# TensorE's overflow branch ahead of the last expert's products, which then stand in both arms

## The reference

```
expert_id = g_top * EXPERTS_PER_GROUP + top_i
combine = jnp.sum(jax.nn.one_hot(expert_id, N_EXPERTS, dtype=jnp.float32) * w[..., None], axis=1)
hid = jax.nn.silu(jnp.einsum('td,edf->etf', t, w_gate)) * jnp.einsum('td,edf->etf', t, w_up)
hid = hid * combine.T.astype(hid.dtype)[:, :, None]
y = jnp.einsum('etf,efd->td', hid, w_down)
x = first_block(...)                      # ends with x + y
return second_block(x, ...)               # begins with rmsnorm(h, g_pre)
```

## Time and profile before

| | |
|---|---|
| median of 3 runs | 1380.82 us (1379.18 to 1384.27) |
| the profiled execution's own time | 1392.52 us |
| its span, first to last instruction | 1391.2 us |
| PE busy / weight loads busy | 1324.2 us (95%) / 800.8 us (58%) |
| DVE / ACT / POOL busy | 571.5 / 338.8 / 477.2 us |
| mean granted TensorE clock | 0.985 |
| matmuls, weight loads | 10076, 10076 |
| the branch | 812.9 us into the span |

### The profile page before, as it was taken

The page is one execution under the profiler, slowest core; times in us unless marked ns, Lnnn a source line. Parts: engine busy times, 40 slices in busy tenths (PEclk is TensorE's granted clock), DMA queues, the critical chain, the costliest instruction groups (busy, mean ns, idle before and its releaser), DMA issues. The chain is left out here.

```text
span 1391.2 us, 24035 instructions
## 1 busy us (share of the span) xinstructions
PE 1324.2 (95%) x10076; PEld 800.8 (58%) x10076; DVE 571.5 (41%) x1381; ACT 338.8 (24%) x788; POOL 477.2 (34%) x586
## 2 busy tenths in 40 slices
PE   6999998999999979999999979999999999999997
PEld 5876445788887454434444425467677445655443
DVE  4366126841415254222111143462388571343315
ACT  2225126631010110111111133462212201322221
POOL 7667603774634800212222302053241011111061
PEclk9999999999999989999999989999999999999999
DMA  8191315021312686999999942011312332200221
GB/s 265 60 382 63 91 61 186 1 65 61 122 61 79 226 302 237 372 360 380 381 378 381 367 176 76 8 61 61 116 67 60 93 106 77 78 2 17 78 105 61
DMA packets 100369, 213.07 MB, mean 153 GB/s; under 512 B 14677, under 2 KB 22704, under 8 KB 100128
## 3 DMA queue, kind: packets, MB, share of 16 engines
q1 hardware_dynamic: 87728, 173.49, 34.9%
q0 software_dynamic: 12528, 37.97, 8.1%
HBM read 190.98 MB, written 19.42 MB: 151 GB/s over the span
## 5 line engine op out<-in xcount | busy, mean ns | idle before, releaser
L1589 POOL TENSOR_TENSOR AR<-Wt,AR 128x512 f32<-128x512 f32 x68 | 88.6, 1323 | 99.1 <-PE pb L1788 93.3
L3932 PE MATMUL pb<-Wt,HT 128*128 128x512 f32 x256 | 117.8, 602 | 0.5 <-DVE AR L4023 0.5
L2480 PE MATMUL pb<-AR 128*64 128x512 f32 x256 | 85.0, 595 | 0.7 <-issue 0.7
L2687 POOL DMA_DIRECT2D ys<-AR x28 | 15.1, 543 | 189.7 <-ACT AR L2651 189.7
L3932 PEld LDWEIGHTS pb<-Wt,HT 128*128 128x128 f32 x256 | 46.3, 190 | 52.4 <-issue 49.3
L1788 PE MATMUL pb<-AR 128*128 128x256 f32 x320 | 73.2, 380 | 1.9 <-DVE AR L1995 1.2
L2480 PE MATMUL pb<-Wt,AR 128*64 128x512 f32 x192 | 70.8, 595 | 0.0
L1788 PEld LDWEIGHTS pb<-AR 128*128 128x128 f32 x320 | 60.2, 190 | 11.5 <-issue 2.0
L1589 POOL TENSOR_TENSOR AR<-Wt 128x512 f32<-128x512 f32 x34 | 44.2, 1320 | 65.1 <-DMA Wt<-in_w_in_dram 30.7
L1788 PE MATMUL pb<-HT,Wt 128*128 128x256 f32 x288 | 65.0, 380 | 0.0
L823 POOL TENSOR_SCALAR X<-X,SM 128x384 f32<-128x384 f32 (+2 forms) x64 | 39.0, 622 | 73.4 <-DVE SM L777 73.4
(11 more groups left out here) (587 smaller groups left out, 2592.1 us busy)
## 6 DMA issues: line engine op xcount, KB each, us to landing
Wt<-in_w_in_dram SPq DMA_DIRECT2D x18, 2048.0 KB, 8.1
AR<-in_w_gate_dram SPq DMA_DIRECT2D x8, 2048.0 KB, 18.1
AR<-in_w_up_dram SPq DMA_DIRECT2D x8, 2048.0 KB, 18.5
AR<-in_w_down_dram SPq DMA_DIRECT2D x8, 2048.0 KB, 17.5
Wt<-in_w_gate_dram SPq DMA_DIRECT2D x6, 2048.0 KB, 18.9
Wt<-in_w_down_dram SPq DMA_DIRECT2D x6, 2048.0 KB, 15.5
Wt<-in_w_up_dram SPq DMA_DIRECT2D x6, 2048.0 KB, 21.2
ys<-AR POOLq DMA_DIRECT2D x2, 3072.0 KB, 25.6
```

Source lines behind the costliest of these rows:

```text
L1589: r = gt.tensor_tensor(out[:, k:k + s, :], a[:, k:k + s, :], b[:, k:k + s, :], op)
L2480: r = mm(s[o:o + 64, :], XT[b % 2][:, k, 0:64], W.ap((n, b))[:, k, :], start=k == 0, stop=k == 7)
L3932: r = mm(s, HT[:, k, t * 128:(t + 1) * 128], W.ap(("gate2", c, br))[:, k, :], start=k == 0, stop=k == 7)
```

## The change

TensorE's `over` is called at the end of `moe_pe` instead of behind it, the loop over steps ends after step 16, and hidden_turn(15) and down(15) become the function `last_expert_pe`. `over` calls it first thing in each arm. Since the two arms are alternatives, the counters of banks and waits are put back before the second one is written. No other engine's program changes.

```diff
+    def state(self):
+        return dict(self.at), list(self.uses), dict(self.table)
+
+    def back_to(self, state):
+        at, uses, table = state
+        self.at, self.uses, self.table = dict(at), list(uses), dict(table)
...
-            for step in range(18):
+            for step in range(17):
...
+            def last_expert_pe():
+                hidden_turn(15)
+                down(15)
+
+            last_expert.append(last_expert_pe)
...
-        def over(e, body):
+        def over(e, body, ahead=None):
 
+            before = P.state(), e.n, dict(e.seen)
             with e.eng.If(count[e.own.name] > 0):
+                if ahead is not None:
+                    ahead()
                 e.eng.drain().then_inc(s_oin, 1)
                 e.eng.wait_ge(s_oin, 4)
                 body()
                 e.eng.drain().then_inc(s_oout, 1)
                 e.eng.wait_ge(s_oout, 4)
             with e.eng.Else():
+                if ahead is not None:
+                    P.back_to(before[0])
+                    e.n, e.seen = before[1:]
+                    ahead()
                 e.eng.sem_inc(s_skip, 1)
...
             moe_pe()
+            over(pe, over_pe, last_expert[0])
...
-        over(pe, over_pe)
```

More of the change, by code:

```diff
@@ L2459, in late_turn_ve @@
                 vt.tensor_copy(flat(x), P.ap(name)).then_inc(P.free(name), 1)
+        last_expert = []
         def moe_pe():
```

## The result

The changed kernel takes 1386.06 us (median of 12 runs, 1383.38 to 1388.89) against 1381.88 us (12 runs, 1379.18 to 1385.34): ratio 1.0029, interval 1.0021 to 1.0037. It is about 4 us slower. The forecast was 1382.1 us, 1.3 us slower, in a range from 1376 to 1387.

A forecast was written before the change was run, and what follows sets the result against it. TensorE, busy 95% of the span, was taken to bound the kernel. Terms +0.2 (late rows' start), -0.4 (clock) and +1.5 (borders) gave +1.3 us over a median of 1380.82: 1382.1 us, range 1376 to 1387.

The forecast's parts named there:

- The mechanism: TensorE's branch: the jump over the overflow body must fetch far code, and its 6.68 us stall moves with the branch.
- my signs of being wrong: Gap ahead of expert 15's transposes under 2 us, or 4 us with the down products behind broken by a second gap.
- The two place terms: Moving the branch: late rows start 0.2 us later (+4.15 against -3.9), and the clock's shift gives -0.4 us.
- The borders: Second block: code lying 106 instructions further along moves stalls at packet borders, +1.5 us, bounds -3 to +3.
- The old place: Ahead of late rows: removing the stall wins 3.9 us and the low clock 2.3, at most 6.2 us together.
- The lead: Ahead of hidden_turn(15): the branch begins 2.9 us before queued work ends, hiding that much; bound 1.45 us.
- The clock at the new place: hidden_turn(15) and down(15): TensorE's 4.1 us stand lowers the clock, losing 1.9 us against 2.3 saved on late rows.
- my 3.4 us of idleness: TensorE: length of standing idle after which the granted clock falls, read from the first profile of before.
- the 3.7 us: Second block: assumed time from one border of 256 instructions until the next code packet can be used.
- The slower rival: New place: code comes late twice, a second stall of up to 3.7 us when down(15) starts; 1388.3 us, chance 0.06.
- Two code packets in the stall: Branch at the new place: if one of the two packets falls outside the stall, it is 2 us shorter; bound only.

The follow-up runs named there:

- e3: Changed kernel without the unexecuted copy of expert 15's products in the first arm, so only the branch's place differs from before: 1386.34 us, ratio 1.0025.
- e9: Kernel before with TensorE's branch turned round at its old place, so the common case falls through and no jump is taken there: 1378.54 us, ratio 0.9972.
- e11: Kernel before with TensorE's overflow body cut from ten blocks to one, so the jump's target is near: 1378.71 us, ratio 0.9969.
- e2: Kernel before, branch at its old place, with only the unexecuted copy of expert 15's transposes and down products added: 1381.64 us, ratio 0.9993.
- e5: Changed kernel with DMA engines kept idle beside the branch (gathers replaced by small copies, SyncE's weight loads delayed): 1383.62 us, ratio 1.0011.
- e6: Kernel before with 3 MB more of DRAM-to-DRAM copies queued behind the gathers, beside the branch at its old place: 1387.3 us, ratio 1.0031.
- e1: Kernel before run once more without any edit, which gave its second profile: ratio 1.0001.
- e4: Changed kernel with the branch moved further ahead, right behind first_rows(15): 1383.34 us, ratio 1.0005 against the kernel before.
- e10: e9 with 160 more semaphore steps on TensorE in first_rows, moving the second block's code borders: 1375.66 us, ratio 0.9960 against the kernel before.
- e7: e4 with 140 more never executed instructions in the first arm, moving the jump's target within its code packet: 1379.69 us, ratio 0.9977.

## Why the forecast held, and where its terms were off

*The mechanism* held: "the stall goes where the branch goes". At the new place nothing hides it but the queue. e3 shows the loss with the place alone, e9 and e11 show that without a far target the branch takes 0.1 to 0.2 us at the old place. Neither of my signs of being wrong came: the gap is 4.96 us, and "ya" and "yb" behind it are whole.

*The number* held in part by luck. 1386.06 us is near the upper end of the range, which I had put there for a second stall that didn't come. The two place terms had -0.2 us, and e3 measures +3.5. The borders had +1.5, and e2 measures -1.0. The two errors go opposite ways.

*The old place* was mis-sized. I took 3.9 us of exposed stall from the row of 6.68 us. In the second profile it is 810.80 - 809.14 = 1.7 us (ScalarE's last copy ended at 807.65 + 1.49). So there was much less to win than the 6.2 us that I had put as the utmost: 1.7 and the low clock on late rows. And I gave the branch one length at both places, where it is 4.35 and 6.25. This step was the largest error of the sum. The page of the Trainium skill that I used (Runtime: NRT & Kernel Launch, Instruction fetch mechanics) says that the fetch is a DMA, and e5 and e6 agree with it (3.65 us against 6.25, 8.52 against 4.35). What stands on the path of that DMA at each place I should have read from the windows.

*The lead.* I expected 2.9 us because the clock was low when down(14) ended. Undisturbed it is full there, and the lead was 1.4 us (799.7 to 801.13). That was my bound, not my value. With 6.25 - 1.4 the gap is 4.96 instead of 4.15.

*The clock at the new place.* Expected loss 1.9 us, measured 6.53 - 3.65 in "ya" and 1.09 - 0.66 in the transposes: 3.3 us. The saving on late rows was 2.75 us in the second profile of before, but e2 has the same gap and full clock behind it:

```profile
811.01 1.96 PE L2893 MATMUL pb<-AR 128*128 128x512 f32 x4 [3.22 <-issue]
```

```profile
811.00:813.00 2.00, 1.99 (x6) 0.76 (x6) 0.00 (x0) 0.00 (x0) 0.00 (x0) 1.00 0.98 369
```

So my 3.4 us of idleness was no length at which the clock falls. It stayed up behind these 3.22 us and fell behind 3.21 in e1 and behind 2.37 in e5. If before pays this loss only in some executions, as e1 and e2 suggest, the saving is smaller on average. The mean granted clock fits that and doesn't prove it: 0.9889 over the runs of before beside e1 to e4, 0.9863 over those of e3, and 0.990 over those of e9 and e10, which have no such gap.

*The sum* from the two undisturbed profiles: 6.6 us later, less 2.75 for late rows, less 0.4 of issue stalls: +3.4 us, against 4.2 measured with an interval of 2.9 to 5.1. The spans of the two differ by 1.0 us only. One reason can be seen in the second block: in e1 the clock is low for 3.4 us behind two of the four stalls, which by an estimate from its level of 0.50 costs 1.7 us each time, and in the changed kernel's profile behind none. One of the two stretches:

```profile
1133.93:1137.34 3.41, 3.31 (x18) 2.60 (x19) 1.52 (x3) 0.00 (x0) 0.54 (x1) 0.50 0.34 63
```

So a stall at a border can cost more than its own length.

*The borders.* I forecast +1.5 us. The number was right: four stalls, each 106 records ahead of a multiple of 256 counted from the stalls of before. The sizes were not: 0.9 to 2.0 us each, 5.5 together, where the count had 7.2. e2 measures the term at -1.0 us (interval -2.3 to +0.3). No row gives the 3.7 us that I took from one border until the next packet can be used. By the trace's start times the 256 instructions before each stall's end took 3.2, 2.9, 3.3 and 3.3 us after the change, so the constant was too large by about 0.5 us for each stall.

*The slower rival* named the right thing at the wrong place: no second stall is seen beside the gap in the changed kernel, but e4 has one of 2.19 us, and e7 removes it by moving the target alone.

*Two code packets in the stall*: the condition of this bound came true, its price did not. One code packet moves during the branch of the changed kernel (starting at 803.55), two during that of e1 (806.17 and 807.08). Yet the branch is 1.9 us longer, not 2 us shorter, and of that time 3.9 us pass before the one packet starts, beside the gathers.

## What to carry to other kernels

A branch whose taken path jumps over a long body costs a code fetch on that engine, and moving it only moves the fetch. Put the common case on the path that falls through, or keep the skipped body short: at the old place, the only one where I ran it, the branch then took 0.09 and 0.24 us. If it has to jump, look at the DMA traffic at the moment of the branch and at the work queued on the engine, not only at which engine waits.

Compare two profiles from a common instruction, and take a second one of the kernel before when one copy or wait in it is several times longer than its neighbours'.

## What the runs showed of the hardware

The compare-and-branch on TensorE took 0.086 us when it fell through and 0.243 us to a target some 120 instructions ahead. To one some 1,200 to 1,300 ahead it took 3.65 us beside idle DMA engines (e5), 4.35 at a share of 0.55 (e1), 6.25 at 0.96 (after the change) and 8.52 at 0.88, with packets of 64 KB in place of 4 KB (e6).

When it began, 34 to 37 matmuls and loads that stand ahead of it had not started, with large matmuls and with small ones. That was 4.4 us of cover in one case and 1.4 in the other.

In straight code, runs of small matmuls at some 7 ns per instruction stopped for 0.6 to 2.6 us at places a multiple of 256 records apart. Unexecuted padding moved these stops and took one away. TensorE went on 1.2 to 1.6 us after the landing of the last code packet at each of these stops, and the far branches ended 1.4 to 1.8 us after it.
